# A hybrid decoder block on 8 cores: key norms one piece behind, more filler matmuls in the last attention slot, the output weight resident

## The chip, the cores and the metric

One Trainium2 chip, all 8 of its cores, one launch. Every core runs the same program on its own rows (cores 0 to 3 one batch element, 4 to 7 the other; a core owns every fourth block of 128 positions, so 2048 rows). Nothing is exchanged between cores. The metric is device time in microseconds of the slowest core.

## The reference

```python
h = rmsnorm(x, norm1_g)
u, q, k, v, gl = split(h @ w_in)
ya = causal_multiscale_pool(u, pool_w, pool_scale) @ w_branch_a
q, k = rmsnorm(q per 64-wide head, q_norm_g), rmsnorm(k per head, k_norm_g)
yb = differential_attention(q, k, v, lam, ...) @ w_branch_b     # causal, ALiBi, 4 heads of 2 maps
g = sigmoid(gl + gate_b)
x = x + (g[0] * ya + g[1] * yb) @ w_out
x = x + square(relu(rmsnorm(x, norm2_g) @ w_ff1)) @ w_ff2
```

SEQ is 8192, D_MODEL 1024, D_FF 4096, 4 heads with two maps of width 64 each and values of width 128.

## The kernel before

The program is written in Python that emits instructions in the order in which each engine is to run them; `Prog.emit` finds the semaphore waits. All instructions leave from one line (L173), so the profile cannot be read by lines: one reads by engine, form and place in time. All five engines are in-order.

**Projection.** 16 groups of 512 positions. `proj_pieces(g)` gives nine pieces: four V pieces (`v_piece`, 8 matmuls of 128x512 and a DVE copy out of PSUM), four K pieces (`k_piece`, 8 matmuls) and one Q piece (`q_piece`, 32 matmuls of 128x128). K and Q are normed per head by `norm_tail`: ScalarE squares the bank, one 128x512 matmul with a block matrix (the "small matmul" below, always into bank 4) sums over each head, ScalarE takes Ln and Exp of it, DVE multiplies. The square is emitted at once; the rest, `fin`, goes into the list `pend` and is emitted later by `flush_pend(keep)`, which keeps the newest `keep`. Between the pieces, `sched_AB` puts the input norm of the next group: four NA parts (`pa`: load x, ScalarE Square with sum, Ln, Exp, then a DVE scaling of the row block into one of two buffers `hbs`) and four NB parts (`pb`, `norm_B`: 8 transposes on TensorE into bank 7 and a DVE copy into `hT`). x has three buffers. Groups 2 and 3 carry a fifth norm (the halo rows).

**Attention.** Slots s = 3, 2, 1, 0 (64, 48, 32, 16 tiles per head, four heads each). Tile i: scores of tile i+2 on TensorE, their Exp on ScalarE, then the products with V of tile i. After each tile `pump(budget)` emits up to BUD[s] filler matmuls from the queue `fq` of groups of the later stages (gates, branches, output projection, pool). All fillers accumulate in bank 7 (`pick`). A group's eviction must have time: `pump` holds the next group back until the counter `pe_ns` has grown by 850 (or 1700 behind a gate); one group per tile at most.

**Drain.** What is left in `fq` when the last tile is done runs now, in the same order, with all eight banks in turn. Its weights come through `ring`, three slots of 8 KB per partition; `seq` is the order of loads: per slot eight `fo` (gate and branch weights, 768 KB each), then `wu` and the two halves of the output weight `wo` (1 MB each). The next load goes into a slot when its last reader is emitted. SyncE issues every load, in order, so one that waits holds up those behind it. `load_w(1, q, i)` loads the four quarters of the second MLP weight, four pieces of 512 KB each; quarter 0 lies over the K and V of groups 0 to 3 (R[0]), the others over later groups and the ring.

**MLP.** Four rounds n of 512 rows: eight `ffn1` pieces (32 matmuls each), then four `ffn2` pieces (64 each) that need the whole second weight; the norm of the next round lies between the `ffn1` pieces, its third and fourth x loads being issued inside.

Of the kernel before, what the change touches and what calls it, by code (L numbers as in the profile page):

```python
# [10 lines left out]
BF16 = mybir.dt.bfloat16  # L11
# [184 lines left out]
def build_nc():  # L196
# [37 lines left out]
    P = Prog()  # L234
    M = Mem()
    es = ExitStack()
    with es:
# [4 lines left out]
                                     "lxr0", "lxr1", "lxr4", "lxr5", "lht0", "ldn0", "ldn1", "ldn2", "ldn3", "sx0", "sx1", "sx2", "sx3", "sx4", "sx5", "ldo0", "ldo1",  # L242
# [113 lines left out]
        def sched_AB(Apieces, NA, NB_, a_at, b_at):  # L356
            for i, a in enumerate(Apieces):
                a()
                for k in range(len(NB_)):
                    if b_at[k] == i:  # L360
                        NB_[k]()
                for k in range(len(NA)):
                    if a_at[k] == i:
                        NA[k]()

        def norm_pieces(srcs):
            NA, NB_ = [], []
            for (src, dst, t_dst, own, gbv_) in srcs:
                st = {}

                def ld(src=src, st=st):
                    st["x"] = ldctr[0] % 3
                    ldctr[0] += 1
                    P.emit("sync", I("dma_start", out=xs[st["x"]], in_=src), writes=[t_xs[st["x"]]], stream=f"ldx{st['x']}")

                def pa(own=own, gbv_=gbv_, st=st, ld=ld):
                    if "x" not in st:
                        ld()
                    x_ = st["x"]
                    k = blkctr[0] % 2  # L380
                    blkctr[0] += 1
                    st["k"] = k
                    lnv, t_l = norm_stats(xs[x_], t_xs[x_], hbs[k], t_hb[k],
                                          None, None)
                    P.emit("dve", I("tensor_scalar", out=hbs[k], in0=xs[x_], scalar1=lnv, scalar2=None, op0=ALU.mult),
                           reads=[t_xs[x_], t_l], writes=[t_hb[k]])

                def pb(dst=dst, t_dst=t_dst, st=st):
                    norm_B(hbs[st["k"]], t_hb[st["k"]], dst, t_dst, 7)
                pa_ld.append(ld)  # L390
                NA.append(pa)
                NB_.append(pb)
            return NA, NB_
# [19 lines left out]
        def proj_pieces(g):  # L413
# [29 lines left out]
            def v_piece(r):  # L443
                def piece():
                    flush_pend(1 if r == 0 else 0)
                    if r == 2:
                        P.emit("sync", I("dma_start", out=hsp[g * 128:(g + 1) * 128, :].rearrange("p (k t) -> p k t", t=128),
                                         in_=hT[:, :, 0:128]), reads=[th[0]], writes=[t_hsp[g]], stream="shs")
                    bi = 5 + r % 2
                    for kc in range(8):  # L450
                        P.emit("pe", I("matmul", bank(bi), lhsT=hT[:, kc, r * 128:(r + 1) * 128], rhs=wv[:, kc, :],
                                       start=(kc == 0), stop=(kc == 7)),
                               reads=[t_wm[0][kc], th[r]], writes=[tb[bi]])
                    P.emit("dve", I("tensor_copy", out=Vg[g][:, r, :].rearrange("p (h e) -> p h e", e=VS)[:, :, 0:128],
                                    in_=bank(bi).rearrange("p (h e) -> p h e", e=128)),
                           reads=[tb[bi]], writes=[t_V[g]])
                return piece

            def k_piece(h):
                def piece():  # L460
# [5 lines left out]
                    flush_pend(1)  # L466
# [3 lines left out]
            def q_piece():  # L470
# [6 lines left out]
                flush_pend(1)  # L477
# [123 lines left out]
        for g in range(NG):  # L601
            A = proj_pieces(g) if g else A_first
            if g + 1 < NG:
                N1, B1 = norm_pieces(group_srcs(g + 1))
            if g == 0:
# [20 lines left out]
            else:  # L626
                A[1] = both(A[1], lambda: flush_pend(1), zero_qz)
# [126 lines left out]
        for s in (3, 2, 1, 0):  # L754
            seq += [("fo", n, s) for n in range(8)]
            seq += [("wu", 0, s), ("wo", 0, s), ("wo", 1, s)] if s > 0 else [("wo", 0, s), ("wo", 1, s)]
# [187 lines left out]
        def grp_out(s, hf, blk, after=None):  # L944
            st = {}

            def mk(kc):
                def f():
                    if kc == 0:
                        st["b"] = pick()  # L950
                    k = slot_of[("wo", hf, s)]
                    P.emit("pe", I("matmul", bank(st["b"]), lhsT=merged[:, kc, blk * 128:(blk + 1) * 128],
                                   rhs=ring[k][:, kc * 512:(kc + 1) * 512], start=(kc == 0), stop=(kc == 7)),
                           reads=[T[f"ring{k}"], T["merged"]], writes=[tb[st["b"]]])
                return f

            def fin():
# [9 lines left out]
                if blk == 3:  # L967
# [373 lines left out]
        BUD = {3: 1, 2: 2, 1: 3, 0: 4}  # L1341
        for i in range(NT):
# [7 lines left out]
            pe_ns[0] += 223 * (4 - tiles[i]["i0"])  # L1350
# [29 lines left out]
        for i in range(4):  # L1380
            sched.setdefault(6 + 5 * i, []).append(lambda i=i: load_w(1, 0, i))
# [67 lines left out]
        for n, s in enumerate((3, 2, 1, 0)):  # L1449
            A = p3b_comp(n, s)  # L1450
            if n + 1 < 4:
                LD_, NA, NB_ = p3b_norm(n + 1, 3 - n - 1)
                if n == 0:
                    LD_[0](); LD_[1]()
                    for q in (1, 2, 3):
                        for j in range(4):
                            load_w(1, q, j)
# [122 lines left out]
```

How the kernel before makes its waits and increments, by code:

```python
        def run(eng):  # L159
            e = engobj[eng]
            for ins in self.q[eng]:
                for d in ins.waits:
                    e.wait_ge(sems[d.stream], val[id(d)])
                r = ins.fn(e)
                if ins.signal:
                    r.then_inc(sems[ins.stream], 16 if ins.stream not in ENGS else 1)
            for d in final_waits.get(eng, ()):
                e.wait_ge(sems[d.stream], val[id(d)])
```

## Time and profile before

| | |
|---|---|
| median of 3 runs | 1674.35 us (1673.52 to 1676.95) |
| the profiled execution | 1673.49 us, span of its slowest core (5) 1671.9 us |
| spans of cores 0 to 7 | 1660.0, 1668.3, 1667.4, 1660.7, 1665.3, 1671.9, 1656.5, 1667.6 us |
| TensorE busy | 1556.6 us (93%) |
| ScalarE, DVE busy | 983.4 us (59%), 639.9 us (38%) |

### The profile page before, as it was taken

To read this page: it belongs to the slowest core of one execution; us is meant where nothing else is said; L and a number is where in the kernel's file an instruction comes from. 1 tells how busy PE (TensorE), PEld (TensorE's weight loads), DVE (VectorE), ACT (ScalarE), POOL (GpSimd) and SP (SyncE) were. 2 spreads that over 40 slices of the span, in tenths; PEclk is the share of its full clock that TensorE was granted. 3 is DMA by queue.
4 is the path that set the end of the run, shared out by engine and by line. 5 is a ranking of instruction groups with operands and counts; after the bars stand their busy time and mean duration, and the time that the engine had idled before them with its cause. 6 is when DMAs were issued, how large, how long until landed. Compare 5 with 4: busy or idle time off the path is not lost.

```text
span 1671.9 us, 33098 instructions; the slowest of 8 cores (1656.5 to 1671.9 us)
## 1 busy us (share of the span) xinstructions
PE 1556.6 (93%) x12112; PEld 955.1 (57%) x12112; DVE 639.9 (38%) x1160; ACT 983.4 (59%) x1399; POOL 65.2 (4%) x109
## 2 busy tenths in 40 slices
PE   5898888899999999999999998888999999999999
PEld 2444444458778887777777776533444444444444
DVE  4565555542430421322333347644543151250320
ACT  6776666669998999888888877521232040130220
POOL 0000000000000000000100001101000000000000
PEclk9999999999999999999999999999999999999999
DMA  9456666317654322335462144465570211201101
GB/s 291 122 139 132 136 137 132 109 58 190 143 115 91 75 61 58 83 95 132 98 158 77 58 140 158 133 222 193 174 255 21 79 54 39 87 26 62 40 16 73
DMA packets 61086, 186.47 MB, mean 112 GB/s; under 512 B 22576, under 2 KB 23216, under 8 KB 56752
## 3 DMA queue, kind: packets, MB, share of 16 engines
q1 hardware_dynamic: 56096, 154.86, 29.8%
q0 software_dynamic: 4832, 29.50, 10.1%
q8 instruction: 100, 1.64, 0.4%
q14 instruction: 58, 0.48, 0.1%
HBM read 179.22 MB, written 47.32 MB: 135 GB/s over the span
## 4 chain that ended last, share of the span: by engine, by line
PE 65%; ACT 17%; issue 6%; DMA 5%; DVE 5%; SPq 1%; ACTq 0%; DVEq 0%; POOL 0%; POOLq 0%
PE psum L173 65%; ACT arena L173 17%; DVE arena L173 5%; DMA arena<-wch 2%; DMA arena<-x1s 1%; DMA arena<-w_qkv 1%; SPq L173 1%; DMA x1s<-arena 1%; ACTq L163 0%; DMA arena<-xkv 0%; DMA arena<-wob 0%; DMA arena<-cst 0%; DVEq L163 0%; POOL arena L173 0%; ACT L173 0%
## 5 line engine op out<-in xcount | busy, mean ns | idle before, releaser
L173 PE MATMUL psum<-arena 128*128 128x129 bf16 (+3 forms) x12112 | 1556.6, 287 | 111.5 <-DVE arena L173 54.0
L173 PEld LDWEIGHTS psum<-arena 128*128 128x128 bf16 x12112 | 955.1, 98 | 712.4 <-issue 185.5
L173 ACT ACTIVATE arena<-psum,arena 128x1024 bf16<-128x1024 f32 (+4 forms) x709 | 638.2, 955 | 169.0 <-PE psum L173 159.3
L173 ACT ACTIVATE arena<-psum 128x512 bf16<-128x512 f32 (+1 forms) x292 | 171.5, 593 | 398.0 <-PE psum L173 370.8
L173 DVE SCALAR_TENSOR_TENSOR arena<-psum,arena 128x512 bf16<-128x512 f32 (+1 forms) x240 | 169.0, 710 | 255.2 <-ACT arena L173 203.3
L173 ACT ACTIVATE arena<-arena 128x1 f32<-128x1 f32 (+3 forms) x314 | 172.4, 562 | 61.9 <-PE psum L173 16.5
L173 DVE COPY arena<-psum 128x1024 bf16<-128x1024 bf16 (+5 forms) x162 | 97.3, 602 | 237.3 <-PE psum L173 235.6
L173 DVE TENSOR_TENSOR arena<-arena 128x512 bf16<-128x512 f32 (+7 forms) x213 | 143.8, 687 | 85.3 <-ACT arena L173 42.1
L173 DVE SCALAR_TENSOR_TENSOR arena<-arena,psum 128x512 f32<-128x512 f32 x64 | 43.5, 687 | 140.6 <-PE psum L173 138.4
L173 DVE TENSOR_TENSOR arena<-psum,arena 128x512 f32<-128x512 f32 x32 | 22.1, 691 | 196.0 <-PE psum L173 196.0
L173 DVE TENSOR_SCALAR arena<-arena 128x1024 bf16<-128x1024 f32 (+3 forms) x123 | 61.5, 502 | 62.7 <-ACT arena L173 57.9
L173 DVE SCALAR_TENSOR_TENSOR arena<-arena 128x128 f32<-128x128 f32 (+3 forms) x98 | 50.5, 517 | 16.0 <-POOL arena L173 9.6
L173 POOL TENSOR_TENSOR arena<-arena 128x4 f32<-128x4 f32 (+1 forms) x32 | 26.3, 822 | 527.9 <-DVE arena L173 527.8
L173 DVE CAST arena<-psum 128x512 bf16<-128x512 f32 x64 | 43.6, 682 | 4.7 <-PE psum L173 4.6
L173 POOL DMA_DIRECT2D w_b<-w x32 | 16.1, 504 | 413.0 <-ACT arena L173 412.6
L173 POOL DMA_DIRECT2D x1s<-arena x32 | 17.8, 556 | 203.1 <-DVE arena L173 190.3
L173 ACT ACTIVATION_READ_ACCUMULATOR arena<-arena 128x1 f32 x82 | 15.4, 188 | 0.0
L173 DVE COPY arena<-arena 64x512 bf16<-64x512 bf16 (+1 forms) x48 | 12.3, 257 | 6.6 <-ACT arena L173 3.9
L173 DVE TENSOR_SCALAR arena<-psum,arena 128x512 bf16<-128x512 f32 x11 | 8.2, 749 | 15.9 <-PE psum L173 15.8
L173 POOL DMA_DIRECT2D wch<-w_abc x4 | 2.2, 560 | 83.0 <-DVE arena L173 83.0
L173 DVE DVE_READ_ACCUMULATOR arena<-arena 128x1 f32 x66 | 5.4, 82 | 0.1
L173 POOL DMA_DIRECT2D wob<-w_oc x4 | 2.0, 490 | 83.4 <-DVE arena L173 83.4
(9 smaller groups left out, 10.6 us busy)
## 6 DMA issues: line engine op xcount, KB each, us to landing
arena<-xkv SPq DMA_DIRECT2D x64, 512.0 KB, 4.8
arena<-wch SPq DMA_DIRECT2D x32, 768.0 KB, 5.8
w_b<-w POOLq DMA_DIRECT2D x32, 512.0 KB, 5.7
arena<-w_b SPq DMA_DIRECT2D x32, 512.0 KB, 9.2
arena<-x1s SPq DMA_DIRECT2D x32, 512.0 KB, 4.2
arena<-w_gc SPq DMA_DIRECT2D x8, 1024.0 KB, 12.7
arena<-xkv SPq DMA_DIRECT2D x32, 256.0 KB, 7.1
arena<-wob SPq DMA_DIRECT2D x8, 1024.0 KB, 6.2
```

The costliest lines, as they stand in the source:

```text
L173: return lambda e: getattr(e, name)(*a, **k)
```

## The change

Five edits. (1) `flush_pend` keeps nothing now: the norm of K piece h is finished right behind the matmuls of piece h+1, that of Q behind V piece 0 of the next group. (2) For the norms emitted in loop steps g = 2 to 14 the scaling is taken out of `pa` and emitted one piece later, behind that piece's NB part (`scales`). (3) There the transposes alternate between bank 4 and bank 7. (4) In attention slot 0 the budget is 8 instead of 4, and each tile adds 1000 to `pe_ns` instead of 223 per block, so that the hold-back of one group ends with the next tile. (5) For slots 1 and 0 the output weight no longer goes through the ring: `load_wo` loads both halves once into R[0], early in the drain; the four loads of quarter 0 of the second MLP weight that stood in the drain go to the MLP's first round, where all 16 loads are spread over its first seven pieces.

```diff
             for i, a in enumerate(Apieces):
                 a()
+                n_sc = len(scales)
                 for k in range(len(NB_)):
                     if b_at[k] == i:
                         NB_[k]()
+                for _ in range(n_sc):
+                    scales.pop(0)()
                 for k in range(len(NA)):
                     if a_at[k] == i:
                         NA[k]()
...
+                    if late[0]:
+                        scales.append(scale)
+                    else:
+                        scale()
...
+                    norm_B(hbs[st["k"]], t_hb[st["k"]], dst, t_dst, 4 if late[0] and tcount[0] % 4 in (1, 3) else 7)
...
             def v_piece(r):
                 def piece():
-                    flush_pend(1 if r == 0 else 0)
...
                            reads=[tb[bi]], writes=[t_V[g]])
+                    flush_pend(0)
...
-                    flush_pend(1)
+                    flush_pend(0)
                     norm_tail(bi, 37, KTg[g][:, h, :], t_KT[g], bank)
...
+            late[0] = g > 1
+            if g > 1:
+                tcount[0] = 0
...
-            seq += [("wu", 0, s), ("wo", 0, s), ("wo", 1, s)] if s > 0 else [("wo", 0, s), ("wo", 1, s)]
+            seq += [("wu", 0, s), ("wo", 0, s), ("wo", 1, s)] if s > 1 else [("wu", 0, s)] if s > 0 else []
+
+        woR = [view(R[0] + 8192 * n, [4096], BF16) for n in range(2)]
+
+        def load_wo():
+            assert not inattn[0]
+            for n in range(2):
+                T[f"wo{n}"] = M.tok(R[0] + 8192 * n, 8192, f"wo{n}")
+                P.emit("sync", I("dma_start", out=woR[n], in_=wob[n * 128:(n + 1) * 128, :]), reads=[t_pco], writes=[T[f"wo{n}"]], stream=f"lwo{n}")
...
-        BUD = {3: 1, 2: 2, 1: 3, 0: 4}
+        BUD = {3: 1, 2: 2, 1: 3, 0: 8}
...
-            pe_ns[0] += 223 * (4 - tiles[i]["i0"])
+            pe_ns[0] += 223 * (4 - tiles[i]["i0"]) if tiles[i]["s"] > 0 else 1000
...
-        for i in range(4):
-            sched.setdefault(6 + 5 * i, []).append(lambda i=i: load_w(1, 0, i))
+        sched[5] = [load_wo]
...
-                    for q in (1, 2, 3):
-                        for j in range(4):
-                            load_w(1, q, j)
+                    ws = [(q, j) for q in range(4) for j in range(4)]
+
+                    def some(n):
+                        def f():
+                            for _ in range(n):
+                                load_w(1, *ws.pop(0))
+                        return f
+                    for i, c in enumerate((3, 3, 3, 2, 2, 2, 1)):
+                        A[i] = both(A[i], some(c))
```

How the instructions stand on TensorE in one group of the steady projection, before, from the small matmul of Q (the first row) to Q's matmuls of the next group (the last). A row of 128x512 is V, K or, alone with a wait for act, a small matmul; 8 rows of 128x128 are one set of transposes.

```order
L173 MATMUL psum<-arena 128x512 [waits act]
L173 MATMUL psum<-arena 128x512 x8
L173 MATMUL psum<-arena 128x512 [waits dve]
L173 MATMUL psum<-arena 128x512 x7
L173 MATMUL psum<-arena 128x128 [waits dve]
L173 MATMUL psum<-arena 128x128 x7
L173 MATMUL psum<-arena 128x512 [waits dve]
L173 MATMUL psum<-arena 128x512 x7
```

The same place leads on, before, from the last transposes over K pieces 2 and 3 (each followed by a small matmul, of the keys two pieces back) to Q, the two small matmuls behind it, and V piece 0:

```order
L173 MATMUL psum<-arena 128x128 x7
L173 MATMUL psum<-arena 128x512 x8
L173 MATMUL psum<-arena 128x512 [waits act]
L173 MATMUL psum<-arena 128x512 x8
L173 MATMUL psum<-arena 128x512 [waits act]
L173 MATMUL psum<-arena 128x128 [waits dve]
L173 MATMUL psum<-arena 128x128 x31
L173 MATMUL psum<-arena 128x512 [waits act] x2
L173 MATMUL psum<-arena 128x512 x8
```

And now, from K piece 1, with one small matmul behind each piece, of the keys one piece back:

```order
L173 MATMUL psum<-arena 128x512 x8
L173 MATMUL psum<-arena 128x512 [waits act,dve]
L173 MATMUL psum<-arena 128x128 [waits dve]
L173 MATMUL psum<-arena 128x128 x7
L173 MATMUL psum<-arena 128x512 x8
L173 MATMUL psum<-arena 128x512 [waits act]
L173 MATMUL psum<-arena 128x512 x8
L173 MATMUL psum<-arena 128x512 [waits act]
L173 MATMUL psum<-arena 128x128 [waits dve]
L173 MATMUL psum<-arena 128x128 x31
L173 MATMUL psum<-arena 128x512 [waits act]
L173 MATMUL psum<-arena 128x512 x8
```

The pair behind Q is gone; there is a small matmul more among the K pieces and one less between Q and V.

SyncE's queue from the end of slot 1's gate and branch groups to the first groups of slot 0 in the drain (wch is an fo load, wub the pool weight, wob a half of the output weight, xkv and x1s rows of x), before:

```order
L173 DMA arena<-wch 128x3072 [waits rg1,pe]
L173 DMA arena<-wub 128x4096 [waits rg2,pe]
L173 DMA arena<-wob 128x4096 [waits rg0,pe]
L173 DMA arena<-wob 128x4096 [waits rg1,pe]
L173 DMA arena<-xkv 128x512 [waits sx0]
L173 DMA arena<-xkv 128x512
L173 DMA arena<-xkv 128x512 [waits dve,sx2]
L173 DMA arena<-wch 128x3072 [waits rg0,pe]
L173 DMA arena<-xkv 128x512 [waits dve,sx3]
L173 DMA arena<-xkv 128x512 [waits dve,sx4]
L173 DMA arena<-xkv 128x512 [waits dve,sx5]
L173 DMA arena<-wch 128x3072 [waits rg2,pe]
```

and now:

```order
L173 DMA arena<-wch 128x3072 [waits rg0,pe]
L173 DMA arena<-wob 128x4096 x2
L173 DMA arena<-wch 128x3072 [waits rg1,pe]
L173 DMA arena<-wub 128x4096 [waits rg2,pe]
L173 DMA arena<-wch 128x3072 [waits rg0,pe]
L173 DMA arena<-x1s 128x1024 [waits ldn2,act,dve]
L173 DMA arena<-wch 128x3072 [waits rg1,pe]
L173 DMA arena<-xkv 128x512 [waits sx0]
```

The two halves of the output weight stand ahead of slot 1's last fo load, and the first two fo loads of slot 0 ahead of the x rows.

## Rows read from the trace of the kernel before

**Rows 1.** The head of the profile's page.

```profile
span 1671.9 us, 33098 instructions; the slowest of 8 cores (1656.5 to 1671.9 us)
```

**Rows 2.** Busy time by stage: projection, slot 0, drain, MLP rounds 0 and 1.

```profile
core 5: us, PE busy (x) PEld busy (x) DVE busy (x) ACT busy (x) POOL busy (x), PEclk, DMA share, GB/s
8.40:366.20 357.80, 312.93 (x2145) 164.76 (x2146) 193.45 (x307) 246.15 (x519) 4.87 (x9) 1.00 0.56 142
...
1006.80:1075.10 68.30, 58.29 (x567) 41.53 (x567) 47.31 (x116) 46.16 (x63) 7.96 (x10) 1.00 0.42 138
1075.10:1216.50 141.40, 123.50 (x580) 55.18 (x578) 67.81 (x116) 30.74 (x48) 11.05 (x20) 0.96 0.61 195
1216.50:1332.90 116.40, 114.16 (x546) 52.52 (x545) 34.68 (x52) 22.92 (x40) 3.08 (x6) 0.99 0.32 109
1332.90:1445.20 112.30, 112.30 (x546) 51.89 (x544) 34.87 (x52) 23.25 (x40) 2.16 (x4) 1.00 0.16 57
```

**Rows 3.** TensorE's timeline in the projection: start, length, count, idle before.

```profile
176.07 6.27 PE L173 MATMUL psum<-arena 128*128 128x512 bf16 x34 [0.89 <-ACT arena L173]
182.83 1.89 PE L173 MATMUL psum<-arena 128*128 128x512 bf16 x8 [0.48 <-DVE arena L173]
185.06 8.84 PE L173 MATMUL psum<-arena 128*128 128x128 bf16 x58 [0.35 <-DVE arena L173]
194.37 2.16 PE L173 MATMUL psum<-arena 128*128 128x128 bf16 x33 [0.47 <-DVE arena L173]
197.43 2.75 PE L173 MATMUL psum<-arena 128*128 128x512 bf16 x12 [0.89 <-ACT arena L173]
```

**Rows 4.** ScalarE and DVE in the same group, same columns.

```profile
185.77 1.06 ACT L173 ACTIVATE arena<-arena 128x1024 bf16<-128x1024 f32 x1 [1.17 <-PE psum L173]
187.49 0.60 ACT L173 ACTIVATE arena<-psum 128x512 bf16<-128x512 f32 x1
187.61 0.75 DVE L173 TENSOR_SCALAR arena<-arena 128x1024 bf16<-128x1024 f32 x1 [0.83 <-ACT arena L173]
192.06 0.60 ACT L173 ACTIVATE arena<-psum 128x512 f32<-128x512 f32 x1 [1.79 <-PE psum L173]
193.28 1.32 ACT L173 ACTIVATE arena<-psum 128x512 bf16<-128x512 f32 x2
```

**Rows 5.** Groups of instructions by form: busy, mean ns of one.

```profile
L173 PE MATMUL psum<-arena 128*128 128x512 bf16 x4320 | 1008.4, 381 | 51.5 <-DVE arena L173 19.4 <-ACT arena L173 17.1 <-DMA arena<-wch 9.2
L173 DVE SCALAR_TENSOR_TENSOR arena<-arena,psum 128x512 f32<-128x512 f32 x64 | 43.5, 687 | 140.6 <-PE psum L173 138.4 <-ACT arena L173 2.1
```

**Rows 6.** DMA issues from 180 to 181.5 us: count, KB, us to landing.

```profile
arena<-xkv SPq DMA_DIRECT2D x1, 512.0 KB, 3.6
```

**Rows 7.** What TensorE waited for in slot 0 (us, times, longest).

```profile
PE psum L173 <- DVE arena L173: 5.7, 10, 1.3
PE psum L173 <- ACT arena L173: 4.1, 10, 0.6
```

**Rows 8.** The same in the drain.

```profile
PE psum L173 <- DMA arena<-wch: 9.2, 4, 5.2
PE psum L173 <- DVE arena L173: 3.1, 2, 1.6
PE psum L173 <- DMA arena<-wob: 2.9, 1, 2.9
PE psum L173 <- ACT arena L173: 2.7, 2, 1.4
```

**Rows 9.** TensorE's timeline in the drain and in MLP round 0.

```profile
1110.22 15.35 PE L173 MATMUL psum<-arena 128*128 128x512 bf16 x64 [2.73 <-DMA arena<-wch]
...
1156.94 5.73 PE L173 MATMUL psum<-arena 128*128 128x512 bf16 x17 [5.20 <-DMA arena<-wch]
...
1252.52 57.76 PE L173 MATMUL psum<-arena 128*128 128x512 bf16 x271 [2.24 <-DVE arena L173]
```

**Rows 10.** DMA issues, 1144 to 1148 us and 1221 to 1229 us.

```profile
arena<-wch SPq DMA_DIRECT2D x1, 768.0 KB, 10.0
...
arena<-w_b SPq DMA_DIRECT2D x12, 512.0 KB, 12.4
```

**Rows 11.** A stretch of the drain at half clock, columns as Rows 2.

```profile
1154.00:1160.80 6.80, 3.86 (x10) 1.42 (x11) 0.00 (x0) 0.19 (x1) 0.00 (x0) 0.50 0.81 302
```

More of the change, by code:

```diff
@@ L241, in build_nc @@
                                      "pcab", "pco", "pcp", "pc1", "pc2", "fst0", "fst1", "fwr0", "fwr1", "lxr2", "lxr3", "lsm", "lwu", "lht", "rg0", "rg1", "rg2",
-                                     "lxr0", "lxr1", "lxr4", "lxr5", "lht0", "ldn0", "ldn1", "ldn2", "ldn3", "sx0", "sx1", "sx2", "sx3", "sx4", "sx5", "ldo0", "ldo1",
+                                     "lxr0", "lxr1", "lxr4", "lxr5", "lht0", "lwo0", "lwo1", "ldn0", "ldn1", "ldn2", "ldn3", "sx0", "sx1", "sx2", "sx3", "sx4", "sx5", "ldo0", "ldo1",
                                      "so0", "so1", "ld_g2", "ld_g1", "ld_sg"] + [f"lf{i}" for i in range(8)]
@@ L364, in sched_AB @@
                         NA[k]()
+        late = [False]
+        scales = []
+        tcount = [0]
         def norm_pieces(srcs):
@@ L384, in pa, with scale @@
                                           None, None)
-                    P.emit("dve", I("tensor_scalar", out=hbs[k], in0=xs[x_], scalar1=lnv, scalar2=None, op0=ALU.mult),
-                           reads=[t_xs[x_], t_l], writes=[t_hb[k]])
+                    def scale():
+                        P.emit("dve", I("tensor_scalar", out=hbs[k], in0=xs[x_], scalar1=lnv, scalar2=None, op0=ALU.mult),
+                               reads=[t_xs[x_], t_l], writes=[t_hb[k]])
+                    if late[0]:
+                        scales.append(scale)
+                    else:
+                        scale()
                 def pb(dst=dst, t_dst=t_dst, st=st):
-                    norm_B(hbs[st["k"]], t_hb[st["k"]], dst, t_dst, 7)
+                    tcount[0] += 1
+                    norm_B(hbs[st["k"]], t_hb[st["k"]], dst, t_dst, 4 if late[0] and tcount[0] % 4 in (1, 3) else 7)
                 pa_ld.append(ld)
@@ L476, in q_piece @@
                                reads=[t_wm[2][kc], th[0]], writes=[tb[bi]])
-                flush_pend(1)
+                flush_pend(0)
                 norm_tail(bi, 36, QT[g // 4][:, :, (g % 4) * 128:(g % 4 + 1) * 128], t_Q[g // 4], None)
@@ L626, in build_nc @@
             else:
-                A[1] = both(A[1], lambda: flush_pend(1), zero_qz)
+                A[1] = both(A[1], zero_qz)
                 A[2] = both(A[2], lambda: make_qz(0, 3, 0))
@@ L950, in f @@
                         st["b"] = pick()
-                    k = slot_of[("wo", hf, s)]
+                    if s > 1:
+                        k = slot_of[("wo", hf, s)]
+                        wv_, tw = ring[k], T[f"ring{k}"]
+                    else:
+                        wv_, tw = woR[hf], T[f"wo{hf}"]
                     P.emit("pe", I("matmul", bank(st["b"]), lhsT=merged[:, kc, blk * 128:(blk + 1) * 128],
-                                   rhs=ring[k][:, kc * 512:(kc + 1) * 512], start=(kc == 0), stop=(kc == 7)),
-                           reads=[T[f"ring{k}"], T["merged"]], writes=[tb[st["b"]]])
+                                   rhs=wv_[:, kc * 512:(kc + 1) * 512], start=(kc == 0), stop=(kc == 7)),
+                           reads=[tw, T["merged"]], writes=[tb[st["b"]]])
                 return f
@@ L966, in fin @@
                        reads=[T[f"xr{k}"]], writes=[t_x1d[s][blk]], stream=f"sx{k}")
-                if blk == 3:
+                if blk == 3 and s > 1:
                     ring_next(slot_of[("wo", hf, s)])
```

## The prediction

> **What bounds the kernel now.** I read the busy time by stage first [rows 1, 2]. TensorE is the bound in every stage: the MLP rounds from 1 on have no gap at all (112.30 of 112.30 us), so the time to be won is what TensorE waits: 44.9 us in the projection, 10.0 in slot 0, 17.9 in the drain, 2.2 in MLP round 0. The rest of attention is not touched. I then read, for each of these, the timeline and the list of waits.
>
> In the projection one group repeats every 21.36 us (176.07 to 197.43), with four waits in it: 0.48 for V's bank, 0.35 for bank 7, 0.47 for Q's bank, which is K piece 0's, 0.89 for the second of two small matmuls in bank 4 [rows 3]. A wait costs more than its gap: matmuls follow at 0.216 us (eight take 1.89, of which the last takes 0.38 [rows 3, 5]), so each gap has a tail of 0.165 before it. The four cost 2.19 + 0.66 = 2.85, and the matmuls themselves need 18.5 us.
>
> In the drain the largest waits are for weights: 9.2 for wch in four pieces, 2.9 for wob [rows 8]. The worst (5.20) ends with a load that took 10.0 us from issue to landing [rows 9, 10], because SyncE's queue had x rows ahead of it. Around it the clock is 0.50 for 6.8 us [rows 11]; the stage's mean is 0.96 [rows 2], so some 11 of its 141 us ran at half clock, and where TensorE worked in them it lost half of that, about 3.6 us.
>
> **Projection: the K side.** ScalarE runs in order. With one piece of lag its queue at K piece h is Ln and Exp of piece h-1, then the square of piece h, and the small matmul behind piece h+1 needs that square. So there is a loop: small matmul 0.38, 0.10 until Ln starts, 1.22 from Ln to the square (192.06 to 193.28), the square 0.59, 0.14 until TensorE goes on: 2.42 us [rows 4, 5]. (The 0.10 and 0.14 are the gaps between a matmul's end and Ln, and between Ln's end and the small matmul, that the timelines show.) TensorE needs 0.22 + 8 x 0.216 = 1.94 between two small matmuls. So behind K piece 3 and behind V piece 0 it waits 0.48 each, behind Q (0.22 + 1.79) 0.41, and behind K piece 2, where a set of transposes (0.44) lies between, 0.04: 1.41 us a group that were not there. In the kernel before the same chain had two pieces, 3.9 us. What goes: the 0.89 (no pair in bank 4) and the 0.47 (piece 0's bank is free a piece earlier).
>
> **Projection: the V side.** Now the first norm's square stands behind Q's Ln and Exp. From the small matmul of Q: Ln at 0.48, norm square at 1.70, its scaling 1.84 later (185.77 to 187.61), at 3.54, done at 4.29, transposes at 4.43 [rows 4]. TensorE wants them after V pieces 1 and 2, at 3.67: 0.76 us of wait. The second set needs a scaling that now stands behind the first set's copy; that comes out even (0.03). The third waits 0.14. The 0.48 goes, because V's copy no longer stands behind two other DVE operations, and the 0.35 goes with the second bank. Sum of the new waits, counted from issue to issue: 1.41 + 0.93 = 2.34 against 2.85, so 0.5 us a group, 5.5 us in the 11 groups of this form. Groups 2 and 3 have a fifth norm in the K side, whose 1.72 us of ScalarE (185.77 to 187.49) now lie in the loop, but their old waits were larger too; groups 0, 1 and 15 swap 0.9 and 0.5 for three or four of 0.48. Both: nothing. **Projection -5.5**, bounds +8 (each loop step 0.2 longer and the halo groups 2 us each) and -16 (no wait at the first transposes, or the loop hidden).
>
> The loads hide: the fourth norm of a group uses the x buffer that the first scaling frees. It is freed at 4.29, the load takes 3.6 [rows 6], so it lands at 7.95; the square could start at 7.35 behind the transposes, and the group feels it only past 8.6.
>
> **Slot 0.** By the order, 29 groups of fillers instead of 13 now run here, 93 more matmuls: 93 x 0.216 = 20.1 us, moved out of the drain, which costs the same here. TensorE's present waits, 9.8 us in 20 places [rows 7], with tails 13.1. What is new: groups now follow each other from tile to tile in bank 7. The last matmul's tail 0.165, 0.1, the eviction 0.69 [rows 5] and 0.14 make 1.1 us, and one tile of slot 0 has 0.2 to 0.9 us of matmuls between. I count 19 such neighbours, 0.57 each: 10.8 us. ScalarE has time in those tiles, so its waits (4.1) go there; they stay in the 35 tiles without filler, some 2 us, as do the head ends, 2.4. New sum 15.2 against 13.1: **+2**, bounds -9 (neighbours free) and +8 (DVE, busy 47 of 68 us, evicts late).
>
> **Drain.** The 5.20 goes: two wch loads of slot 0 are issued before the x rows, some 20 us ahead of use. The 2.9 goes, as the output weight lands long before. So do about 0.9 of the 1.3 us of small wch waits (9.2 less 5.2 and 2.7) and the ACT wait of 1.4 [rows 8], whose groups have moved. The 2.73 at 1110.22 [rows 9] is slot 1's fo load 6 or 7, and it gets worse: both halves of the output weight, 2 MB, are issued right behind load 6 and 5 us ahead of load 7. At 302 GB/s [rows 11] 2.1 MB are 7 us and load 7's 0.8 MB 2.6. Counted from the drain's start, load 6 is issued at 1.9 and lands near 8, wob near 11.5 and 15, load 7 near 18; TensorE wants it at 13.4 or so. I take 5 us of wait there and 0.7 for load 6; bounds 1 (shared evenly) and 8. What a late load 7 delays next is wub, wanted 7 us later, which then just comes. New DMA waits 6.1 against 12.1: -6. ACT and DVE -1.4, four tails -0.6, half clock: one such stretch is left of three, -1.7. **Drain -9.5**, bounds -16 and -2, beside the 20.1 that moved.
>
> The Trainium skill (DMA: Bandwidth & Descriptors, section Queues, rings and completion order) says that each DMA engine takes descriptors in the order of its ring, yet that completion is not first in, first out by issuing engine. By the first half the sum above stands; were the two halves to share evenly with load 7, the wait would be near 1 us and the time 4 us less. This trace's twelve queued loads took 12.4 us in the median [rows 10], which speaks for the order.
>
> **MLP round 0.** Quarter 0's loads come in, but of the 12 loads that stood ahead of the third x load 9 are left. Half a MB at 302 GB/s [rows 11] is 1.7 us, and the 12 landed 12.4 us after issue in the median [rows 10], one behind the other; three fewer let x land some 5 us earlier, and the 2.24 us wait at 1252.52 [rows 9] goes with the stretch at half clock behind it: 116.4 to 112.4, **-4.0 on core 5**. The whole second weight, 16 x 1.7 = 28 us of transfer, starts with the round; `ffn2` begins after 8 x 32 x 0.216 = 55 us. Cores that had no such wait (core 7) gain nothing.
>
> **The sum.** Core 5: 1671.9 - 5.5 + 2 - 9.5 - 4.0 = 1654.9. Core 1 (1668.3, 1 us to gain in the MLP, 8 in the drain) comes to 1655.8, core 7 to 1655. The slowest near 1655.5, and 1.6 around the span: 1657 us. This is against 1673.49 of the profiled execution, 0.9 under the median; the clock's stretches fall differently from run to run, so I leave it there.
>
> **The rivals.**
> - *The loads of the output weight cost what the ring gave* (0.15): load 7 waits 8 us, wub comes late too, one more stretch at half clock. Drain -2 instead of -9.5: 1664. For it: the 10.0 us row. Against: most of it lands under 12 us of matmuls.
> - *The fillers fill* (0.12): bank 7's evictions are no wait, because DVE is free and the scores stand between; slot 0 grows by 11 instead of 22: 1646.
> - *The norm chains are hidden* (0.08): no loop on the K side and no late scaling; 2.3 more in each of 13 groups: 1627. Against it stands the loop of 2.42 us.
> - *The fourth x load is caught* (0.06), the other side: the cast transfers of the branch weights (groups 3 to 11) are issued by GpSimd when V piece 3 is copied, at 7.6 us on the clock above, and the fourth load should land at 7.95. If they stretch it to the 10.0 us that a load in a full queue took [rows 10], the chain of square, K norm and small matmul is 5.6 us late in 8 groups: +45 us, 1702. It decides past 8.6; below that it costs nothing. With 2.5 us of delay in each it would already be slower than before.
> - *Nothing comes of it* (0.05): projection +8, slot 0 +5, drain -9: within 3 us of 1674.
>
> **How the numbers follow.** My own case has 0.54, at 1650 to 1662. The range leaves out the hidden chains and the caught load: 1645 to 1667. A measurement tells 0.2%, 3.3 us, from no change. Faster: 0.54 + 0.15 + 0.12 + 0.08 and a part of the last, 0.90; same 0.03; slower 0.07.
>
> **What would show it.** In the steady projection a period of 20.8 us, with waits for ACT of 0.3 to 0.5 in front of small matmuls (three a group) and one for DVE of 0.6 in front of the first transposes. Slot 0 near 90 us. In the drain one wch wait of about 5 us near its 12th us and none before slot 0's gates. Round 0 at 112.4 us on every core. Wrong: a period over 21.3, or x loads of 512 KB over 4.5 us where the first scaling frees them; a slot 0 over 96 us; a wait for wub.

## The result: 0.23 % slower, where 1 % faster was forecast

| | before | changed |
|---|---|---|
| median, same chip | 1675.38 us | 1679.85 us |
| ratio of times, 95 % interval | | 1.0023 [1.0013, 1.0033] |
| the profiled execution | 1673.49 us (span 1671.9) | 1676.58 us (span 1675.0) |
| projection, mean of cores (least to most) | 358.0 (356.6 to 359.7) | 362.8 (361.5 to 364.3) |
| attention slot 0 | 69.5 (68.4 to 70.0) | 100.7 (100.1 to 101.3) |
| drain | 138.9 (134.0 to 142.1) | 109.6 (107.5 to 111.6) |
| MLP round 0 | 115.3 (112.5 to 117.6) | 112.6 (112.4 to 113.2) |

The lower four rows are the lengths of the stages on TensorE, from the traces of the profiled executions, over the six cores whose matmul records are complete. They add up to +4.0 us, the ratio to +3.9. The medians here and below are of all executions, while the ratios and the profiles leave out those in which the cores of one die or of both ran at a lower clock. The forecast was 1657 with a range from 1645 to 1667; the time lies 13 us above that range. The stages tell where: 97 matmuls (661 now against 564 in slot 0) went from the drain into slot 0, 97 x 0.216 = 21.0 us. Without them slot 0 is **10.2** longer (forecast 2), the drain **8.3** shorter (9.5), MLP round 0 **2.7** shorter (4.0 on the slowest core), and the projection **4.8 longer** (5.5 shorter). Of the 21 us between forecast and time 10.3 lie in the projection, 8.2 in slot 0 and 2.5 in the other two.

### The profile page after: what moved, and what is told of

It reads as the page before. It is cut to its first block, busy times and chain, and to the rows that moved or that the text cites. A ratio compares the mean times of both kernels' runs of the same rounds, so it can differ in the third digit from the quotient of the medians.

```text
span 1675.0 us, 33082 instructions; the slowest of 8 cores (1665.4 to 1675.0 us)
## 1 busy us (share of the span) xinstructions
PE 1561.7 (93%) x12112; PEld 953.3 (57%) x12112; DVE 640.7 (38%) x1161; ACT 982.4 (59%) x1398; POOL 67.5 (4%) x109
## 4 chain that ended last, share of the span: by engine, by line
PE 68%; ACT 19%; issue 5%; DVE 4%; DMA 3%; ACTq 0%; SPq 0%; DVEq 0%
PE psum L173 68%; ACT arena L173 19%; DVE arena L173 4%; DMA arena<-xkv 2%; DMA arena<-wch 1%; DMA arena<-wub 1%; ACTq L163 0%; DMA wch<-arena 0%; SPq L173 0%; DVEq L163 0%; ACT L173 0%; SPq L163 0%
## 5 line engine op out<-in xcount | busy, mean ns | idle before, releaser
L173 PE MATMUL psum<-arena 128*128 128x512 bf16 (+3 forms) x12112 | 1561.7, 287 | 109.5 <-ACT arena L173 53.3
L173 ACT ACTIVATE arena<-psum 128x512 f32<-128x512 f32 (+1 forms) x292 | 172.6, 592 | 398.3 <-PE psum L173 363.8
L173 ACT ACTIVATE arena<-arena 128x1 f32<-128x1 f32 (+4 forms) x314 | 172.5, 562 | 64.3 <-DMA arena<-xkv 22.9
L173 DVE SCALAR_TENSOR_TENSOR arena<-arena 128x128 f32<-128x128 f32 (+3 forms) x98 | 50.5, 516 | 17.0 <-POOL arena L173 10.3
L173 POOL DMA_DIRECT2D x1s<-arena x32 | 17.7, 554 | 177.7 <-DVE arena L173 165.0
```

The costliest lines, as they stand in the source:

```text
L173: return lambda e: getattr(e, name)(*a, **k)
```

## The profile after

The page's head, and the windows by stage on core 2, the slowest: projection, slot 0, drain, MLP rounds 0 and 1, as [rows 1, 2].

```profile
span 1675.0 us, 33082 instructions; the slowest of 8 cores (1665.4 to 1675.0 us)
```

```profile
core 2: us, PE busy (x) PEld busy (x) DVE busy (x) ACT busy (x) POOL busy (x), PEclk, DMA share, GB/s
9.10:372.60 363.50, 319.05 (x2146) 163.61 (x2147) 194.68 (x307) 245.70 (x519) 7.25 (x9) 0.99 0.50 140
1011.10:1112.20 101.10, 83.36 (x663) 52.32 (x661) 54.19 (x125) 51.34 (x71) 7.77 (x10) 0.97 0.38 131
1112.20:1223.60 111.40, 100.49 (x484) 45.43 (x482) 60.86 (x106) 24.69 (x39) 10.99 (x20) 0.98 0.54 178
1223.60:1336.00 112.40, 112.40 (x546) 51.99 (x545) 34.59 (x52) 22.92 (x40) 3.17 (x6) 1.00 0.39 132
1336.00:1448.30 112.30, 112.30 (x546) 51.89 (x544) 34.87 (x52) 23.25 (x40) 2.17 (x4) 1.00 0.17 57
```

MLP round 0 has no gap left, and the drain waits 10.9 us where it waited 17.9. The projection still has 44.5 us without TensorE at work, as before; slot 0 has 17.7 instead of 10.0.

**The projection.** TensorE's timeline in two places: the two groups with a halo norm in them, then one steady group, as [rows 3].

```profile
70.25 3.83 PE L173 MATMUL psum<-arena 128*128 128x512 bf16 x17 [0.65 <-ACT arena L173]
76.46 12.86 PE L173 MATMUL psum<-arena 128*128 128x128 bf16 x74 [2.38 <-ACT arena L173]
90.53 0.38 PE L173 MATMUL psum<-arena 128*128 128x512 bf16 x1 [1.22 <-ACT arena L173]
91.80 4.34 PE L173 MATMUL psum<-arena 128*128 128x128 bf16 x49 [0.89 <-ACT arena L173]
96.52 3.83 PE L173 MATMUL psum<-arena 128*128 128x512 bf16 x17 [0.37 <-ACT arena L173]
...
114.65 0.38 PE L173 MATMUL psum<-arena 128*128 128x512 bf16 x1 [1.48 <-ACT arena L173]
115.92 4.34 PE L173 MATMUL psum<-arena 128*128 128x128 bf16 x49 [0.89 <-ACT arena L173]
120.64 3.83 PE L173 MATMUL psum<-arena 128*128 128x512 bf16 x17 [0.37 <-ACT arena L173]
...
182.24 2.10 PE L173 MATMUL psum<-arena 128*128 128x512 bf16 x9 [0.31 <-ACT arena L173]
184.71 3.83 PE L173 MATMUL psum<-arena 128*128 128x512 bf16 x17 [0.37 <-ACT arena L173]
189.30 11.30 PE L173 MATMUL psum<-arena 128*128 128x128 bf16 x74 [0.76 <-ACT arena L173]
200.92 2.16 PE L173 MATMUL psum<-arena 128*128 128x512 bf16 x33 [0.32 <-ACT arena L173]
203.40 2.10 PE L173 MATMUL psum<-arena 128*128 128x512 bf16 x9 [0.31 <-ACT arena L173]
```

From group 2 on nearly every wait now ends with ScalarE. In the steady group there are four: 0.31 behind Q, 0.37 behind V piece 0, 0.76 before the first transposes, 0.32 behind K piece 3; a group without a disturbance takes 21.16 us (from 182.24 to 203.40), against 21.36. Where the fifth norm lies in the K side, small matmuls wait 1.22, 1.48 and twice 0.89, and the period, from behind one V piece 0 to behind the next, is 26.27 and then 24.12 us.

ScalarE in the loop: Ln at 198.97, Exp at 199.66, the square at 200.20, which ends at 200.78; TensorE goes on at 200.92.

```profile
198.97 0.60 ACT L173 ACTIVATE arena<-psum 128x512 f32<-128x512 f32 x1 [0.62 <-PE psum L173]
199.66 0.63 ACT L173 ACTIVATE arena<-arena 128x512 f32<-128x512 f32 x1
200.20 0.58 ACT L173 ACTIVATE arena<-psum 128x512 bf16<-128x512 f32 x1
```

**Slot 0.** What TensorE waited for, as [rows 7]:

```profile
PE psum L173 <- DVE arena L173: 13.9, 24, 1.9
PE psum L173 <- ACT arena L173: 3.5, 9, 0.6
```

Its timeline over three tiles with fillers and some without, and the DVE eviction between two of them:

```profile
1042.59 2.55 PE L173 MATMUL psum<-arena 128*128 128x512 bf16 x16 [0.35 <-DVE arena L173]
1045.49 4.46 PE L173 MATMUL psum<-arena 128*128 128x512 bf16 x41 [0.35 <-DVE arena L173]
1050.23 0.27 PE L173 MATMUL psum<-arena 128*128 128x256 bf16 x1 [0.28 <-ACT arena L173]
1051.03 1.39 PE L173 MATMUL psum<-arena 128*128 128x129 bf16 x19 [0.53 <-DVE arena L173]
1052.75 0.93 PE L173 MATMUL psum<-arena 128*128 128x256 bf16 x9 [0.33 <-ACT arena L173]
```

```profile
1044.65 0.69 DVE L173 SCALAR_TENSOR_TENSOR arena<-psum,arena 128x512 f32<-128x512 f32 x1 [2.13 <-PE psum L173]
```

DVE begins to empty bank 7 at 1044.65, TensorE has a few matmuls for other banks until 1045.14, DVE is done at 1045.34 and the next group starts at 1045.49: the neighbours of the forecast, one tile every 2.90 us. On core 2, 19 waits stand right before a filler group, as many as were counted. But the waits for ScalarE and for the head's end are mostly still there: 9 for ScalarE with 3.5 us, where there were 10 with 4.1 [rows 7].

**The drain.** Waits as [rows 8], and the DMA issues from 1112 to 1122 us (count, KB each, median us to landing):

```profile
PE psum L173 <- DVE arena L173: 6.0, 4, 2.3
PE psum L173 <- DMA arena<-wch: 3.6, 1, 3.6
PE psum L173 <- ACT arena L173: 1.3, 1, 1.3
```

```profile
arena<-wob SPq DMA_DIRECT2D x2, 1024.0 KB, 9.3
arena<-wch SPq DMA_DIRECT2D x2, 768.0 KB, 8.0
```

Of 12.1 us of waits for weights 3.6 are left by the profile's names, in one piece, at slot 1's last fo load. The waits for DVE have grown, from 3.1 in two places to 6.0 in four; one of them, 1.1, is in truth slot 1's load 6 (below).

## The experiments

Ratios are to the kernel before on the same chip; stage lengths are means of six cores.

| kernel | median us | ratio [95 %] | projection | slot 0 | drain | MLP 0 |
|---|---|---|---|---|---|---|
| e123_proj_only | 1682.23 | 1.0031 [1.0019, 1.0043] | 363.1 | 69.9 | 137.1 | 114.5 |
| e1_flush_only | 1682.59 | 1.0035 [1.0019, 1.0051] | 363.5 | 70.0 | 137.8 | 114.0 |
| e1_square_first | 1658.6 | 0.9898 [0.9876, 0.9921] | 341.4 | 70.0 | 138.3 | 115.8 |
| e4_fillers_only | 1684.14 | 1.0047 [1.0032, 1.0062] | 358.9 | 100.4 | 116.6 | 118.8 |
| e5_wo_only | 1660.25 | 0.9903 [0.9886, 0.992] | 358.1 | 69.6 | 127.8 | 112.5 |
| e5_spread_only | 1666.93 | 0.9975 [0.9962, 0.9987] | 357.1 | 69.7 | 134.4 | 112.5 |
| e5_fill_gap | 1655.08 | 0.9869 [0.9847, 0.9892] | 358.3 | 72.8 | 121.7 | 112.4 |
| best_wo_square | 1643.53 | 0.9799 [0.9775, 0.9822] | 340.8 | 69.8 | 127.8 | 112.4 |
| best_plus_late | 1645.51 | 0.9809 [0.9787, 0.9831] | 342.6 | 69.5 | 128.1 | 112.4 |
| after_square_first | 1659.75 | 0.9923 [0.9907, 0.9938] | 342.1 | 100.7 | 108.8 | 112.4 |
| after_no_fillers | 1663.04 | 0.9947 [0.9931, 0.9963] | 362.7 | 69.9 | 128.8 | 112.5 |
| best_all | 1636.81 | 0.9793 [0.9777, 0.9808] | 339.2 | 72.9 | 121.6 | 112.5 |

### One part at a time

**e123_proj_only**: edits 1 to 3 (all of the projection's) on the kernel before, 4 and 5 left out.

> The kernel before with the three projection edits alone (lag of one piece, scaling one piece later, transposes in two banks). Theory A, that these edits cost more in groups 0 to 3 than they give later: the projection 4 to 6 us longer on every core, the steady period 21.16 us against 21.36, the end of group 3 some 5 us late, the time 4 to 5 us above the kernel before. Theory B, that the late projection of the changed kernel comes from something else (other clock stretches, SyncE's queue): the projection within 1 us of before.

Projection +5.1, the other stages as before: the loss of the projection belongs to these edits, whatever the rest does.

**e1_square_first**: edit 1 alone, with the new square put ahead of the Ln and Exp of the piece before:

```diff
-                    flush_pend(1)
                     norm_tail(bi, 37, KTg[g][:, h, :], t_KT[g], bank)
+                    flush_pend(1)
```

(and the same for Q; V pieces as in the change).

> The kernel before with the lag of one piece alone, and the square of piece h emitted ahead of Ln and Exp of piece h-1 instead of behind them. TensorE's order is that of the changed kernel. Theory A, that ScalarE's order closes a loop of 2.42 us around the small matmul: with the square first the loop is open, no small matmul waits for ScalarE, the waits of 0.89 and 0.47 of before are gone too, the period is 19.6 to 19.9 us and the time 18 to 22 us below the kernel before. Theory B, that the small matmul waits for the Ln of the last one in bank 4: the waits of 0.3 to 0.4 stay, period 21 us, time within 3 us of before.

Here `flush_pend(1)` stands behind the `norm_tail` that adds a new entry, so that it keeps only this one: the lag is still one piece. The projection is 16.6 us shorter than before and 22 shorter than with the order of the change; the time is 17 us less by the ratio, a little under the 18 of theory A. TensorE's timeline and ScalarE's in the steady group:

```profile
179.09 2.49 PE L173 MATMUL psum<-arena 128*128 128x128 bf16 x16 [0.53 <-DVE arena L173]
181.92 16.57 PE L173 MATMUL psum<-arena 128*128 128x128 bf16 x117 [0.34 <-DVE arena L173]
199.02 2.49 PE L173 MATMUL psum<-arena 128*128 128x128 bf16 x16 [0.53 <-DVE arena L173]
```

```profile
208.84 1.09 ACT L173 ACTIVATE arena<-psum 128x512 bf16<-128x512 f32 x2 [0.58 <-PE psum L173]
210.02 0.63 ACT L173 ACTIVATE arena<-arena 128x512 f32<-128x512 f32 x1
```

The pair at 208.84 is the square of a piece and, right behind it, the Ln of the piece before; Exp comes last. No small matmul waits any more: two waits are left in place of four, both for DVE before transposes, and the period is 19.93 us (179.09 to 199.02) against 21.36. So one piece of lag is worth 1.43 us a group, and what takes it away in the change is that the square stands behind Ln and Exp.

**e4_fillers_only**: edit 4 alone (budget 8, 1000 per tile).

> The kernel before with the filler edit of slot 0 alone. Theory A, that fillers from tile to tile wait for bank 7 while the waits of the scores and of the products with V stay: slot 0 is 30 to 33 us longer, the drain 21 to 24 shorter, the time 7 to 11 us above. Theory B, that the drain gains more than the matmuls moved because its waits for weights go with them: slot 0 30 longer, drain 30 shorter, no change.

Its windows for slot 0, drain and MLP round 0 on the slowest core:

```profile
1013.40:1113.80 100.40, 83.77 (x664) 53.01 (x663) 54.36 (x126) 51.60 (x71) 7.76 (x10) 0.97 0.39 133
1113.80:1228.60 114.80, 102.34 (x484) 45.77 (x482) 60.93 (x106) 24.70 (x39) 10.85 (x19) 0.97 0.66 210
1228.60:1348.80 120.20, 114.69 (x546) 52.65 (x545) 34.70 (x52) 22.98 (x40) 3.26 (x6) 0.97 0.34 106
```

Slot 0 is 30.9 longer for 21.0 us of matmuls, the drain 22.3 shorter, MLP round 0 3.5 longer. The fillers alone make the kernel slower, by 0.47 %, as theory A has it.

**e5_wo_only**: edit 5 alone, the resident output weight and the spread loads.

> The kernel before with the output weight resident and the 16 weight loads in the MLP's first round, alone. Theory A, that these loads are what the changed kernel gains by: the drain 5 to 8 us shorter (the wob wait and the 5.2 us wch wait gone, one new wch wait of 2 to 4 us behind the 2 MB), MLP round 0 at 112.4 us on every core, the time 6 to 11 us below. Theory B, that the drain's gain came from the fillers that moved out: drain as before, time 2 to 4 us below by round 0 alone.

The drain is 11.1 us shorter and MLP round 0 2.8; the time is 16 us less, more than either theory allowed. Windows of slot 0, drain and MLP round 0, and the drain's waits:

```profile
1009.70:1077.90 68.20, 58.16 (x567) 41.45 (x566) 47.28 (x116) 46.12 (x63) 7.96 (x10) 1.00 0.41 139
1077.90:1205.40 127.50, 120.10 (x580) 54.55 (x578) 67.88 (x116) 30.73 (x48) 11.08 (x20) 1.00 0.58 184
1205.40:1317.80 112.40, 112.40 (x546) 51.89 (x545) 34.61 (x52) 22.92 (x40) 3.06 (x6) 1.00 0.40 131
```

```profile
PE psum L173 <- DVE arena L173: 3.4, 3, 1.6
PE psum L173 <- ACT arena L173: 2.7, 2, 1.4
PE psum L173 <- DMA arena<-wch: 1.2, 2, 0.9
```

Of 12.1 us of waits for weights [rows 8] 1.2 are left, and the granted clock of the stage is 1.00 where it was 0.96 [rows 2]: for 580 matmul records TensorE was busy 120.10 us, before 123.50.

**e5_spread_only**: the second half of that edit alone. The four loads of quarter 0 leave the drain, all 16 are spread over MLP round 0, and the output weight still comes through the ring.

> The kernel before with the second half of edit 5 alone: the four loads of quarter 0 of the second MLP weight go from the drain to the first MLP round, where all 16 loads are spread over seven pieces; the output weight still comes through the ring. Theory A, the spread saves only the wait of MLP round 0, and the resident output weight saves the drain's: MLP round 0 at 112.5, drain 134 to 142 as before, time 1670 to 1673. Theory B, the four 512 KB loads in the middle of the drain were what made its weights late: drain 126 to 131, time 1660 to 1665.

Neither theory: MLP round 0 has 112.5 in the mean, as theory A has it, but the drain, 134.4 in the mean, runs from 130.0 to 137.7 over the cores, between the two, and the time is under theory A's. So the spread is worth 4.5 us in the drain and both halves together 11.1. The resident weight was not run alone; by the difference it is the larger half (0.9903 for both, 0.9975 for the spread).

### What the scaling and the banks do, and where the loss sits

**e1_flush_only**: edit 1 alone, as the change has it.

> The kernel before with the lag of one piece alone, the square behind Ln and Exp as in the changed kernel. Theory A, that the loop on ScalarE and what it does in groups 0 to 3 is the whole loss of the projection edits: ACT waits of 0.3 to 0.4 behind K pieces 3, Q and V piece 0, groups 0 to 3 together 4 to 6 us longer, the projection 3 to 6 us longer. Theory B, that the later scaling and the second bank make the loss in groups 2 and 3: the projection within 1.5 us of before or shorter, groups 0 and 1 still 1 to 2 us longer.

363.5 against 363.1 for all three projection edits: edit 1 alone loses as much as the three. In the sum the later scaling and the two banks change nothing that these runs can tell. By groups they do two things, which cancel. The table has the times between the starts of Q's matmuls, means of six cores, read from the traces:

| kernel | start to group 1 | group 2 | group 3 | groups 4 to 14 |
|---|---|---|---|---|
| before | 55.1 | 24.2 | 21.4 | 235.3 |
| changed | 56.7 | 25.8 | 24.2 | 233.5 |
| e123_proj_only | 56.6 | 25.8 | 24.3 | 233.8 |
| e1_flush_only | 56.4 | 24.8 | 22.6 | 237.0 |
| best_wo_square | 57.9 | 22.7 | 20.9 | 220.3 |
| best_plus_late | 57.2 | 25.2 | 23.4 | 217.7 |

Against e1_flush_only the two edits win 3.2 us in the eleven groups of the steady form and lose 2.7 in groups 2 and 3, where the fifth norm lies.

**best_wo_square**: edit 5, and edit 1 with the square first.

> The kernel before with the lag of one piece, the square ahead of Ln and Exp, and the output weight resident with the loads in the MLP's first round; neither the later scaling nor the two banks nor the filler edit. Theory A, that the two gains lie in different stages and add: 1642 us, 1.9 to 2.1% under the kernel before, projection 340 to 343 us, drain 127 to 129, MLP round 0 at 112.4. Theory B, that the parts share a common limit (the slower stretches of the clock or the transfers): 1650 us.

The gains add up: 0.9898 x 0.9903 = 0.9802, measured 0.9799.

**best_plus_late**: the same with edits 2 and 3.

> The same with the scaling one piece later and the transposes in two banks for the norms of loop steps 2 to 14, as in the changed kernel. Theory A, that with the loop open these two edits trade the DVE waits of 0.53 and 0.34 before the transposes for one of 0.76: 0.3 us a group less, the projection 1 to 4 us shorter. Theory B, that the later scaling lays a wait into each group that the banks do not pay for: the projection 2 to 8 us longer.

Projection 342.6 against 340.8. In a steady group TensorE waits some 0.6 us, in one piece of 0.63 or in two of 0.31 and 0.29, where best_wo_square waits 0.53 and 0.34, and the period is 19.65 us against 19.93: there theory A holds, 0.3 us less a group. Groups 2 and 3 lose 5.0 us (the table), which is more than the eleven groups give back (2.6). The intervals of the two times overlap, so it is no gain, and not shown to be a loss. The two edits in the groups without a fifth norm alone were not run.

**after_square_first**: the changed kernel, only the square put first.

> The changed kernel with one thing put otherwise: the new square is emitted ahead of the Ln and Exp of the piece before, so that a small matmul no longer waits for Ln, Exp and square in a row. Theory A, this loop on ScalarE is the whole loss of the projection: the projection is 18 to 23 us shorter than in the changed kernel, slot 0 stays at 100 and the drain at 108 to 112, time 1655 to 1662. Theory B, the scaling one piece later, the two banks or the halo groups are what the projection waits for: 0 to 8 us shorter, time 1672 to 1680.

Projection 342.1, which is 20.7 less than in the changed kernel, every other stage as there. The order of two lines decides over the sign of the whole change.

### The fillers

**after_no_fillers**: the changed kernel with budget 4 and 223 per block.

> The changed kernel without its fourth edit: the budget in slot 0 is 4 again and each tile adds 223 per block. Theory A, the parts add up: 1682.2 less the 16 of edit 5 = 1664 to 1668, slot 0 at 70, drain 127 to 130, so that the fillers alone cost the changed kernel 12 to 16 us. Theory B, the waits that the fillers bring into slot 0 are paid back by weights that come in time in the drain: 1676 to 1681, drain 135 or more.

Slot 0 goes from 100.7 back to 69.9, the drain from 109.6 to 128.8: the fillers cost the changed kernel 11.6 us by stages, and 12.7 by the ratios (1.0023 less 0.9947): theory A. By stages that is what they cost alone (30.9 - 22.3 + 3.5 = 12.1); the ratio of e4_fillers_only says 7.9, since its profiled execution, 1689.63 us, was above its median. The drain shrinks by 19.2 for 21.0 us of matmuls taken out: none of the waits in slot 0 is paid back there.

**e5_fill_gap**: edits 4 and 5 on the kernel before, with a longer hold-back in slot 0, so that no two groups stand in neighbouring tiles:

```diff
-                    ready[0] = pe_ns[0] + (850 if g["gap"] == 1 else 1700)
+                    ready[0] = pe_ns[0] + ((850 if tile_no[0] < starts[12] else 1050) if g["gap"] == 1 else 1700)
```

> The resident output weight as in e5_wo_only, and in slot 0 eight fillers a tile with 1000 added a tile as in the changed kernel, but the hold-back raised from 850 to 1050, so that one tile always lies between two groups; 29 matmuls more in slot 0 than before instead of 97. Theory A, that the cost of the filler edit is the eviction of bank 7 from tile to tile: no waits of fillers above 0.2 us, slot 0 6 to 8 us longer, the time within 2 us of e5_wo_only. Theory B, that matmuls in slot 0 cost more than in the drain whatever their spacing, since the scores' and V products' waits stay: slot 0 9 to 12 us longer, the time 3 to 5 us above e5_wo_only.

Again neither theory. 29 matmuls (593 against 564), 6.3 us, moved into slot 0; it grew by only 3.2 over e5_wo_only, and the drain lost 6.1. TensorE's waits in slot 0 on core 0:

```profile
PE psum L173 <- DVE arena L173: 5.1, 8, 1.4
PE psum L173 <- ACT arena L173: 2.7, 9, 0.5
```

Together 7.8 us in 17 places, where there were 9.8 in 20 [rows 7]; 5 of the 17, with 2.2 us, stand right before a filler group. So these fillers do fill waits of slot 0, as a rival of the prediction had it. That the spacing is what lets them, and not their smaller number, is my reading: no run has 97 fillers with a second bank. By the times the gain over e5_wo_only is 0.34 %, and the two intervals just touch.

**best_all**: edit 5, the square first, the spaced fillers.

> The resident output weight and the spread loads (edit 5) in the kernel before, the key norms one piece behind with the square placed ahead of Ln and Exp, and the budget of 8 in slot 0 with a hold-back of 1050 behind each group of fillers, so that two groups never follow each other in bank 7 in neighbouring tiles. Theory A, the three parts lie in different stages and add up: 1643.5 less the 4 to 5 that the spaced fillers gave = 1637 to 1640, projection ending near 342 to 350, slot 0 at 72 to 73, drain 120 to 124. Theory B, the gain of the spaced fillers was a matter of how that run's loads fell: 1642 to 1645, drain 125 or more.

```profile
span 1635.7 us, 33003 instructions; the slowest of 8 cores (1626.8 to 1635.7 us)
```

The stages came as theory A said. By the ratios it is not told apart from best_wo_square (0.9793 and 0.9799); its slot 0 and drain together are 3.1 us shorter (72.9 + 121.6 against 69.8 + 127.8). It is 2.1 % faster than the kernel before and 2.3 % faster than the changed one.

## Why the prediction was wrong

**"So 0.5 us a group, 5.5 us in the 11 groups of this form"**: three times too large. The four large waits came close to the working: 0.32, 0.31, 0.37 and 0.76, which with a tail of 0.165 each are 0.48, 0.48, 0.54 and 0.92, for 0.48, 0.41, 0.48 and 0.76. The three small ones are there too, in the starts of the single matmul records, too short to show as idle because the matmul before is still under way: 0.03, 0.11 and 0.16 us for 0.04, 0.03 and 0.14. Together 2.7 for the 2.34 of the sum, against 2.9 before. And some groups take 0.3 to 0.6 more. From group to group the changed kernel won 0.16, some 1.7 in all.

**"Both: nothing"**, of groups 0 to 3 and 15: this is the step that failed most. In the mean of six cores groups 0 and 1 are 1.6 us longer, group 2 1.6, group 3 2.8 and group 15 0.5 (the table above), 6.5 us that stood in no term. Followed by the start of Q's matmuls, core 5 was 2.3 us behind the kernel before in group 1, 4.1 in group 2 and 6.9 in group 3 and then won back some 0.15 a group. Group 1 carries no fifth norm: on core 5 five waits, 2.6 us together, lie there between the starts of Q's matmuls of group 0 and of group 1, where there were two, 1.5 together. Putting the square first wins nothing back there (57.9 in the table), and no run tells more of the cause. I had written that the old waits of groups 2 and 3 were larger too. For group 2 that holds, but group 3 took 21.35 us before (90.67 to 112.02), as a steady one, and takes 24.12 now: the norm's Square, Ln and Exp lie inside the loop, and nothing was there to be swapped. The bound of +8 for the projection had the halo groups ("2 us each"), and measured was +4.8; I gave it no weight in the value taken.

**The loop itself** was seen and priced, and then put down as the cost of the lag. It is the cost of an order: the square needs only its own piece's bank and could stand first. After_square_first shows it: 20.7 us.

**Slot 0, "ScalarE has time in those tiles, so its waits (4.1) go there"**: wrong. The neighbours cost about what was forecast: the 19 waits at the filler groups took 10.5 us on core 2, 13.6 with their tails, forecast 10.8. But the other waits, of scores and V products, are 6.9 us in 14 places, 9.2 with tails, of 9.8 in 20 and 13.1 before [rows 7], where 4.4 were to be left. My reading, which no run isolates, is that ScalarE's chain in an unfilled tile starts with that tile's scores, so that the time it has in a filled tile before is of no use to it. On core 5 slot 0 is 11.5 us longer beside the 21.0 of matmuls: waits 17.0 instead of 10.0, 13 more tails 2.1, and a rest of 2.4, which I put down to matmuls at half clock for the most part (below). That is past the bound of +8 that the forecast gave this step. Without either miss, this one or that of "Both: nothing", the changed kernel would have come out faster.

**Drain and MLP round 0** were right, in size and in mechanism, though the drain's terms add up to -9.7 and not -9.5. Core 5's drain went from 141.4 to 111.0 us, which is 9.4 beside the 21.0 that moved. The forecast put the two halves of the output weight at 11.5 and 15 us after the drain's start, load 7 near 18 with 5 us of wait. The trace has 10.4, 13.2 and 17.1 (issued at 1119.31, landed at 1129.26), and 3.6 of wait; the wait of 1.11 that ends at 1120.33, where the profile names DVE, is slot 1's load 6, which landed at 1120.09; forecast 0.7. What was off is the count of matmuls moved, 97 for 93, the waits for DVE, put at no more than before, and the cores: the mean of the drain was 2.5 below core 5's already, so there was less to be won. The Trainium skill (DMA: Bandwidth & Descriptors, Queues, rings and completion order) says that on each DMA engine the descriptors of a ring are consumed in its order. The trace agrees: load 7, issued 4.3 us behind the second half, took 9.96 us and landed 3.8 behind it.

**The chances.** The faster side got 0.90. My own upper bounds, +8 in the projection, +8 in slot 0, -2 in the drain and -4 in MLP round 0, sum to +10. Measured was +4.8, +10.2, -8.3 and -2.7: two bad ends at once. Only one rival had both, "Nothing comes of it", with +8 in the projection, +5 in slot 0 and -9 in the drain. It came nearest, and it had 0.05.

## What to carry to other kernels

When work is pipelined one step tighter on an in-order engine, write down the queue of that engine for one period and look at what stands ahead of the operation that the bound engine waits for: put the operation that needs nothing of the previous step first. Fillers for a waiting engine need a gap between two groups, or a second buffer, which no run here tries; without it each brought a wait of its own and left most of the old ones. A period read from steady groups says nothing about the groups that carry extra work; read their period before as well.

## What the runs showed of the hardware that was not expected

TensorE's clock is at half for longer in slot 0 once it is full of fillers. Windows on core 2 around such a place:

```profile
1044.00:1050.00 6.00, 5.53 (x52) 3.75 (x49) 2.87 (x5) 3.15 (x4) 1.23 (x2) 1.00 0.49 136
1050.00:1056.80 6.80, 3.39 (x34) 2.39 (x35) 5.66 (x10) 4.35 (x8) 0.00 (x0) 0.93 0.67 268
1056.80:1062.30 5.50, 5.46 (x23) 2.80 (x24) 2.12 (x5) 0.90 (x1) 0.00 (x0) 0.50 0.00 0
```

Ahead of the fall lie the unfilled tiles at a head's end, in which TensorE was busy half of the time, in short pieces; then 5.5 us at 1.2 GHz, in which it was busy all the time with 23 matmuls. Slot 0 is not free of it before: there five of the six cores have 3.4 us at half clock in it (core 5, the slowest, has none); now all six have 6.8, and in e5_fill_gap none of six has any. At half speed while TensorE works, 6.8 us cost up to 3.4, and the 4.0 us more in the mean up to 2.0 of slot 0's 10.2: an estimate. The Trainium skill (TensorE: Matmul & The Clock Gate, A second HAM failure mode: psum-queue depth-cycling) describes short idle times between groups of matmuls that cycle through banks as a reason for such swings. The short idle times are in this trace (3.39 us of work in 6.80), though the fillers do not cycle through banks but all use bank 7; no run isolates the cause. In the drain the effect works the other way: with fewer waits for weights (e5_wo_only) the stage's clock went from 0.96 to 1.00, on all six cores without any time at half clock where each had 3.4 to 10.2 us before, and this is a part of why edit 5 gave 16 us where the waits that went were 10.5 in the drain (17.9 to 7.4) and 2.2 in MLP round 0.
